# Four small changes of order in a four-layer encoder kernel: sums, low parts, weight splits and squares at the joints, and one product in two runs

## What is computed

```python
for i in range(DEPTH):                       # 4 layers
    h = _rmsnorm(x, attn_norm[i])
    if i % 3 == 0:   x = x + stick_breaking_mixer(h, ...)
    elif i % 3 == 1: x = x + mla_mixer(h, ...)           # latent attention
    else:            x = x + swa_sink_mixer(h, ...)      # sliding window
    x = x + swiglu_ffn(_rmsnorm(x, ffn_norm[i]), ...)
return _rmsnorm(x, final_norm)

def swiglu_ffn(h, w_gate, w_up, w_down):
    return (jax.nn.silu(h @ w_gate) * (h @ w_up)) @ w_down
```

## Time and profile before

| | |
|---|---|
| median of 3 runs | 1200.11 us (1200.05 to 1200.42) |
| the profiled execution | 1201.47 us, span 1199.7 us |
| mean granted clock of TensorE | 0.995 of full speed |
| busy TensorE / VectorE / ScalarE / GpSimd | 98% / 67% / 53% / 24% |
| instructions in the span | 18306 |
| bytes moved by DMA | 201.85 MB, mean 168 GB/s |

### The profile page before, as it was taken

How to read it: one execution, slowest core, us unless ns; L and a number is a source line. 1 busy time by engine, 2 the same in 40 slices (tenths; PEclk the granted TensorE clock), 3 DMA queues, 4 the chain that set the end, 5 groups by cost and what they waited for, 6 DMA issues and landing times.

```text
span 1199.7 us, 18306 instructions
## 1 busy us (share of the span) xinstructions
PE 1177.0 (98%) x7410; PEld 1045.0 (87%) x7410; DVE 807.7 (67%) x873; ACT 632.6 (53%) x803; POOL 286.6 (24%) x290
## 2 busy tenths in 40 slices
PE   8999999999999999999999999999999999999996
PEld 6989888888997888888899888888889988888885
DVE  7686776766597467766556577667556868677653
ACT  5675555553346545555336555555436755555531
POOL 5000532211123253221111173221110005422221
PEclk9999999999999999999999999999999999999999
DMA  8733445565553145555553255555545335455541
GB/s 318 213 118 106 176 176 208 178 207 179 186 164 106 67 148 213 182 201 203 184 176 106 72 175 206 181 208 182 193 158 202 111 106 176 176 185 187 197 169 35
DMA packets 30830, 201.85 MB, mean 168 GB/s; under 512 B 3505, under 2 KB 4593, under 8 KB 7329
## 3 DMA queue, kind: packets, MB, share of 16 engines
q1 hardware_dynamic: 28800, 197.41, 47.0%
q0 software_dynamic: 352, 1.31, 0.9%
q10 hardware_dynamic: 1600, 2.02, 0.7%
HBM read 197.91 MB, written 1.84 MB: 166 GB/s over the span
## 4 chain that ended last, share of the span: by engine, by line
PE 88%; DVE 8%; ACT 3%; issue 0%; DMA 0%; ACTq 0%; DVEq 0%
PE banks L1186 39%; PE banks L1190 21%; PE banks L1180 6%; PE banks L1182 5%; PE banks L1181 5%; PE banks L1174 4%; DVE w_lo L764 3%; DVE x_split L779 2%; PE banks L1257 2%; ACT w_hi L441 1%; PE banks L1315 1%; PE banks L1329 1%; PE banks L1545 1%; DVE w_lo L773 1%; PE banks L1472 1%; PE banks L1259 1%
## 5 line engine op out<-in xcount | busy, mean ns | idle before, releaser
L764 DVE TENSOR_TENSOR w_lo<-raw,w_hi 128x2048 fp32r<-128x2048 f32 x183 | 449.9, 2459 | 214.9 <-ACT w_hi L441 214.8
L441 ACT ACTIVATE w_hi<-raw 128x2048 fp32r<-128x2048 f32 x183 | 349.3, 1909 | 95.5 <-PE banks L1190 47.2
L1186 PE MATMUL banks<-x_split,w_hi 128*128 128x512 f32 x1408 | 338.8, 392 | 5.2 <-DVE x_split L779 5.2
L1186 PEld LDWEIGHTS banks<-x_split,w_hi 128*128 128x128 f32 x1408 | 258.4, 188 | 58.0 <-DVE x_split L779 8.2
L1190 PEld LDWEIGHTS banks<-x_split,w_lo 128*128 128x128 f32 x1408 | 181.9, 193 | 7.0
L1190 PE MATMUL banks<-x_split,w_lo 128*128 128x256 f32 x1408 | 184.0, 284 | 0.0
L1186 PE MATMUL banks<-hid_split,w_hi 128*128 128x512 f32 x704 | 173.2, 392 | 0.0
L1186 PEld LDWEIGHTS banks<-hid_split,w_hi 128*128 128x128 f32 x704 | 127.4, 188 | 23.3
L1180 PE MATMUL banks<-x_split,w_hi 128*128 128x256 f32 x384 | 110.3, 287 | 0.0
L1181 PE MATMUL banks<-x_split,w_hi 128*128 128x256 f32 x384 | 108.6, 283 | 0.0
L1182 PE MATMUL banks<-x_split,w_lo 128*128 128x256 f32 x384 | 108.6, 283 | 0.0
(11 more groups left out here) (174 smaller groups left out, 1498.3 us busy)
## 6 DMA issues: line engine op xcount, KB each, us to landing
raw<-w SPq DMA_DIRECT2D x183, 1024.0 KB, 4.8
raw<-w SPq DMA_DIRECT2D x8, 256.0 KB, 6.6
x<-x_in SPq DMA_DIRECT2D x2, 512.0 KB, 5.5
raw<-w SPq DMA_DIRECT2D x2, 512.0 KB, 9.2
out<-x SPq DMA_DIRECT2D x4, 256.0 KB, 2.8
k_all<-k_all ACTq DMA_DIRECT2D x1, 960.0 KB, 7.7
rel_scratch<-rel_lut POOLq DMA_DIRECT2D x1, 768.0 KB, 10.6
rel_bias<-rel_scratch POOLq DMA_DIRECT2D x2, 256.0 KB, 8.5
```

Of the source, the lines that this page charges most:

```text
L441: act.activation(w_hi[slot][:, :], raw[slot][:, :], ACT.Copy).then_inc(hi_done, 1)
L764: dve.tensor_tensor(w_lo[slot][:, :], raw[slot][:, :], w_hi[slot][:, :].bitcast(FP32), ALU.subtract).then_inc(lo_done, 1)
L1186: return pe.matmul(pair(b), wt[0], xs, start=first, stop=False, skip_group_check=True)
```

## The change

It has four parts.

1. VectorE, `out_projection`, in all four layers: the split of the first up unit moves from ahead of the low part of tile 4 to behind the low part of tile 7.
2. GpSimd, `model_squares` of the four SwiGLU norms: the squares of tiles 4 to 7 wait until all eight low parts are made.
3. TensorE, `two_halves` of the first gate unit in each layer: tiles 0 to 5 high, then low, then tiles 6 and 7 high, then low.
4. VectorE, `latent_attention`: the mean square of the queries moves ahead of the first keys, and the fourth pair of queries from behind the first two maxima to behind the third pair, ahead of a split.

```diff
--- before.py
+++ after.py
@@ -315,7 +315,7 @@
                     if n == 0:
                         pool.wait_ge(x_loaded[k // 4], 16)
                     elif n < NORMS - 1:
-                        pool.wait_ge(norm.lo, 8 * n + k + 1)
+                        pool.wait_ge(norm.lo, 8 * n + (KT if n % 2 and k >= 4 else k + 1))
                     else:
                         pool.wait_ge(norm.x_new, 8 * (n - 1) + k + 1)
                     dst = sq_sum if k == 0 else sq
@@ -825,13 +825,13 @@
                 norm_lo(n, 3)
                 add(4)
                 add(5)
-                split(u + SPLIT_SLOTS + 2)
                 norm_lo(n, 4)
                 norm_lo(n, 5)
                 add(6)
                 norm_lo(n, 6)
                 add(7)
                 norm_lo(n, 7)
+                split(u + SPLIT_SLOTS + 2)
                 split(u + SPLIT_SLOTS + 3)
 
             def out_lo(m, dst, src, hi):
@@ -940,10 +940,10 @@
                     dve.tensor_tensor(q_all[:, 2 * r:2 * r + 2, :], pair(MLA_Q_BANKS[r]), both(rope_q[:, :]),
                                       ALU.mult).then_inc(m.q_new, 1)
 
-                keys(0)
                 dve.wait_ge(c.sums, 2)
                 dve.tensor_scalar(ms[:, 0:SEQ], bank[1][:, 0:SEQ], 1.0 / Q_RANK, EPS, ALU.mult,
                                   ALU.add).then_inc(c.ms, 1)
+                keys(0)
                 keys(1)
                 refine(c, 2, 0, SEQ, rstd_c)
                 dve.tensor_tensor(rope_q[:, :], rstd_c[:, 0:SEQ], table[:, C_QROPE:C_QROPE + SEQ],
@@ -952,7 +952,7 @@
                 keys(2)
                 keys(3)
                 dve.wait_ge(m.rope_tab, 2)
-                for r in range(3):
+                for r in range(4):
                     queries(r)
                 split(b + 7)
 
@@ -981,7 +981,6 @@
 
                 maxima(0)
                 maxima(1)
-                queries(3)
                 inverse(0)
                 inverse(1)
                 queries(4)
@@ -1601,14 +1600,15 @@
 
                 def two_halves(u, first_bank, new):
                     pe.wait_ge(lo_done, u + 1)
-                    for k in range(KT):
-                        if new:
-                            pe.wait_ge(norm.lo, 8 * n + k + 1)
-                        for a in range(2):
-                            high_halves(first_bank + a, w_tile(u % 3, a * KT + k), x_tile(k), k == 0)
-                    for k in range(KT):
-                        for a in range(2):
-                            last = low_half(first_bank + a, w_tile(u % 3, a * KT + k), x_tile(k), k == KT - 1)
+                    for run in (range(0, 6), range(6, KT)) if new else (range(KT),):
+                        for k in run:
+                            if new:
+                                pe.wait_ge(norm.lo, 8 * n + k + 1)
+                            for a in range(2):
+                                high_halves(first_bank + a, w_tile(u % 3, a * KT + k), x_tile(k), k == 0)
+                        for k in run:
+                            for a in range(2):
+                                last = low_half(first_bank + a, w_tile(u % 3, a * KT + k), x_tile(k), k == KT - 1)
                     last.then_inc(unit_used, 1)
 
                 for c in range(FFN_CHUNKS):
```

## The result

The changed kernel takes **1208.62 us** (median of 6 runs, 1206.75 to 1212.01) against 1200.09 us (6 runs, 1200.00 to 1200.42): a ratio of 1.007 with a 95% interval of 1.006 to 1.008. Its profiled execution took 1212.01 us, span 1209.9, and is the slowest of the six. The scatter itself is new: 5 us, where the kernel before had 0.4 us in those runs.

A forecast was written before the change was run, and what follows sets the result against it. TensorE, busy 1177.0 of 1199.7 us, bounds the kernel, so only its waits matter. From the median, joints and latent layer (+3.2 us) give 1203.3; two clock falls add 3.0: 1206.3 us, range 1199.5 to 1210.0.

The forecast's parts named there:

- the third case: Rival: GpSimd is not held up by all three splits, so faster, 1196.2 or 1191.6 us; chance 0.20.
- the fourth: Rival: low parts of tiles 6 and 7 stay late, little moves, 1199 to 1202 us; 0.12 with mixed cases.
- Low parts earlier (part 1): First gate units: TensorE's seven waits for low parts of x vanish, freeing 7.3 us over four joints.
- Squares later (part 2): SwiGLU norms: splits hold GpSimd up, squares' product 1.0 us later in three joints, 1.4 us in the third.
- joint: The place of the first gate unit behind each attention mixer; there are four, one in each layer.
- Who gets the port: VectorE's third split goes ahead of GpSimd's sum; the skill's issue-first rule would put the product 0.2 us earlier per joint.
- the row with a lead of 0.23 us: Third joint before the change: GpSimd's record began 0.23 us ahead of the split, yet lasted 2.99 us.
- Latent layer (part 4): Latent attention: TensorE's two waits go, one of 0.3 us comes before the first transpose; gain 1.2 us, bounds 0.3 to 1.9.
- The waits' net: Whole kernel without falls in the joints: 3 x 1.0 + 1.4 - 1.2 = +3.2 us.
- The clock: Behind TensorE's new waits in the joints: granted clock falls to 0.50, 1.5 us each; two falls taken, 3.0 us.
- Median or profiled execution: Baseline: profiled execution lies 1.36 us above the median 1200.11, nearly one fall, so the median counts as without one.

The follow-up runs named there:

- one split fewer in GpSimd's way: The changed kernel with the third split moved behind the mean square on VectorE: 1197.32 us, ratio 0.9969.
- the filler: The changed kernel with 24 spare bf16 products on TensorE ahead of the squares' product: 1203.49 us, ratio 1.0025.
- the first four experiments: On the kernel before: parts 1, 3 and 4 without part 2, 1194.78 us; part 2 alone, 1207.27; part 3 alone, 1196.91; part 1 alone, 1196.48.
- part 2 alone: Only the late squares of tiles 4 to 7, on the kernel before: 1207.27 us, ratio 1.0055.
- part 4 alone: Only the new order in the latent layer, on the kernel before: 1200.02 us, ratio interval 0.9982 to 1.0002.

## Why the prediction was right

The forecast was 1206.3 us in 1199.5 to 1210.0, measured 1208.6, for the reason given; two of the six executions, 1211.66 and 1212.01, lie above the range. The sentence that gives the range says that it takes in the third case. It doesn't, with 1196.2 and 1191.6 us: what it reaches down to is the fourth. Point by point:

- **Low parts earlier (part 1).** The low part of tile 7 ended at 132.77 in the trace (forecast 132.8). All seven waits went.
- **Squares later (part 2).** From the gate unit's start to the squares' product 14.13 us were measured against 14.2 forecast, and 715.25 - 701.61 = 13.6 in the third joint, whose gate unit began at 701.61, against 13.7. The square of tile 4 ended at 135.45, its sum at 138.20 and the sum of tile 5 at 141.85, against 135.52, 138.14 and 141.8 forecast. It is shown, not only argued, that part 2 does it: with it alone +6.9 us, without it -5.6, and one split fewer in GpSimd's way took 10.7 us of wait to 2.5. One of the four waits, the third joint's 2.32 us, is shorter than the 2.5 to 3.1 that I had named.
- **Who gets the port.** I had preferred the row with a lead of 0.23 us to the Trainium skill's rule (SBUF — State Buffer, "Who interferes with whom"). In the first joint of the trace GpSimd's sum began 0.01 us behind the third split, so both say the same there and it doesn't decide between them. But my preference rested on one row, and others speak against it. In the earlier trace rows GpSimd's first square began 0.22 us ahead of the split at 123.39 and went first: it took 0.78 us and the split 2.70. In the change's third joint the sum of tile 5 began 0.26 us ahead of the split and went first, as I had taken it for that joint:

```profile
709.56 0.73 POOL L326 TENSOR_TENSOR sq_sum<-sq_sum,sq 128x256 f32<-128x256 f32 x1
...
709.82 2.62 DVE L764 TENSOR_TENSOR w_lo<-raw,w_hi 128x2048 fp32r<-128x2048 f32 x1 [1.04 <-ACT w_hi L441]
```

So leads of 0.22 and 0.23 us in the records ended one way and the other, and a lead of this size doesn't say who goes first. What does stays open.

- **Latent layer (part 4).** 1.2 us forecast, 1.3 measured in kernels without falls, with the wait of 0.6 us before the first transpose.
- **The waits' net.** +3.2 us forecast, +3.3 with the filler.
- **The clock (part 4 of the text, "a fall costs 1.5 us; I take two").** This term was too small: 3.0 us against 5.1. The profiled execution had a fall in each joint. Between the squares' product and the gate unit's low products the second joint took 7.00 us where the kernel before took 4.09 (438.70 to 442.79), and the fourth 1029.90 - 1022.78 = 7.12: about 3 us each, not 1.5, since the clock stayed down longer: from 438.5 to 445 in the rows above, where the kernel before was below full clock in that joint only between 429 and 433. The first and third lost 1.7 and 1.5 us. This is the slowest of the executions; in the median the falls cost 5.1.
- **Median or profiled execution.** I took the 1.36 us between the two as one fall. Its 23 later runs fit that: 15 lie from 1199.8 to 1200.7, 8 from 1201.4 to 1202.0, and none between. Another 14 do the same (9 and 5). Of the 12 beside the first four experiments, however, 1200.91 and 1201.25 lie between, so the gap isn't always there, and only one execution of this kernel was profiled.

## What to carry to other kernels

When a helper engine's small operations can't run beside another engine's long ones, count how many long operations lie between their start and the moment their result is wanted; delaying the small ones to favour the big one's critical steps can move them into a much worse neighbourhood. When a wait ahead of TensorE is taken away, TensorE asks for the next thing that much earlier, so cost that next thing (here the squares' sum, with 0.06 us to spare in one joint) before the edit. And a wait of a few microseconds on TensorE is to be priced with the clock that it may lose behind it, which here was more than the wait.

## What the runs showed of the hardware

- Useless products in place of an idle stretch of 2.8 us made the kernel 5.1 us faster; the profiled execution has no stretch at half clock in a joint, where that of the change has four. I had expected a fall to be likely, not that the falls would outweigh the waits.
- A fall is not a matter of the wait alone: part 2 alone waits up to 1.7 us at a stretch for the sum, after two shorter ones, and its profiled execution shows no fall in a joint; the kernel before waits 1.5 us in two pieces and falls in some executions. Kernels whose waits in the joints are 0.7 us or less scatter by 0.3 to 1.4 us; the kernel before and part 4 alone, with two waits of 0.7 and 0.8 us close together, by about 2 and by 3.5; the change, with 2.3 and 2.8 us, by 5.3; but part 2 alone, with 1.7 us, only by 1.1. The length of a wait doesn't order them, and what does was not tested.
- Behind the low part of tile 7 GpSimd and VectorE's splits took turns: in the first joint of the change two splits took 4.90 us instead of the 4.58 of two free ones, and GpSimd got one operation in between, never two.
